# A fused two-block transformer kernel: block outputs on strips of 32 rows and seven pieces of work reordered in its second stage

## The reference

```python
q, gl, mq = split_cols(h @ w_in, [512, 24, 512])       # h: norm of x
k_c, v_c, k_s, v_s, k_w, v_w = rmsnorm(x, g_kv) @ w_kv
k_cmp, v_cmp = (gelu(blocks(a) @ w1) @ w2 for a in (k_c, v_c))   # 15 blocks, 2 groups
o = g0 * softmax(q k_cmp) v_cmp + g1 * softmax(q k_s) v_s + g2 * softmax(q k_w) v_w
m = softmax(mq mem_k) mem_v                            # 4 heads
x = x + concat([o, m]) @ w_out
```

## Time and profile before

| what | value |
|---|---|
| median of 3 runs | 894.53 us (894.26 to 894.65) |
| profiled execution, its own time | 893.82 us |
| span of its records | 892.1 us |
| TensorE busy | 885.8 us (99%) |
| VectorE busy | 648.7 us (73%) |
| ScalarE busy | 495.4 us (56%) |
| GpSimd busy | 44.3 us (5%) |

### The profile page before, as it was taken

One profiled execution on the slowest core, in us unless ns is written; L12 is line 12 of the kernel. 1 busy time (PEld: TensorE's weight loads), 2 busy tenths in 40 slices (PEclk: granted clock), 3 DMA queues, 4 the chain that ended last, 5 costly groups with the idle time before them and its releaser, 6 DMA issues.

```text
span 892.1 us, 18697 instructions
## 1 busy us (share of the span) xinstructions
PE 885.8 (99%) x7883; PEld 861.4 (97%) x7883; DVE 648.7 (73%) x1189; ACT 495.4 (56%) x851; POOL 44.3 (5%) x54
## 2 busy tenths in 40 slices
PE   8999999999999999999999999999999999999998
PEld 7999999999999998889999999999988999999998
DVE  6997657887767789785887767678688586565664
ACT  6763566564545566575565546547457464444451
POOL 1000001000000001000100000001142000000000
PEclk9999999999999999999999999999999999999999
DMA  8753343565465544632546554553162265546541
GB/s 324 287 189 113 126 174 134 211 243 190 155 227 187 187 151 160 242 124 97 213 181 243 205 200 176 213 211 129 64 235 96 96 228 201 195 181 217 199 152 48
DMA packets 26002, 160.68 MB, mean 180 GB/s; under 512 B 3008, under 2 KB 4928, under 8 KB 7360
## 3 DMA queue, kind: packets, MB, share of 16 engines
q1 hardware_dynamic: 25344, 158.45, 48.7%
q10 hardware_dynamic: 576, 1.05, 0.4%
HBM read 158.18 MB, written 1.05 MB: 178 GB/s over the span
## 4 chain that ended last, share of the span: by engine, by line
PE 94%; DVE 4%; ACT 1%; DMA 1%; issue 0%; SPq 0%
PE ps L417 92%; PE ps L433 2%; DVE wl L1291 1%; DMA xt<-in_x 1%; DVE xl L1299 1%; DVE arena L1741 0%; ACT coh L2097 0%; ACT wh L2085 0%; DVE xt L1487 0%; DVE col L1299 0%; ACT arena L2105 0%; DVE arena L1330 0%; DVE arena L1725 0%; DVE arena L1797 0%; DVE wl L1507 0%
## 5 line engine op out<-in xcount | busy, mean ns | idle before, releaser
L1291 DVE TENSOR_TENSOR wl<-raw,wh 128x1024 fp32r<-128x1024 f32 x280 | 329.5, 1224 | 120.8 <-ACT wh L2085 120.4
L417 PE MATMUL ps<-xh,wh 128*128 128x256 f32 (+1 forms) x1256 | 349.3, 278 | 0.6 <-DVE wl L1507 0.6
L417 PE MATMUL ps<-xl,wh 128*128 128x256 f32 (+1 forms) x1256 | 347.6, 277 | 0.0
L417 PE MATMUL ps<-xh,wl 128*128 128x256 f32 (+1 forms) x1256 | 347.6, 277 | 0.0
L2085 ACT CAST wh<-raw 128x1024 fp32r<-128x1024 f32 x280 | 277.3, 1048 | 115.3 <-PE ps L417 105.1
L417 PEld LDWEIGHTS ps<-xh,wh 128*128 128x128 f32 x1256 | 235.9, 188 | 2.0 <-DVE wl L1507 1.2
L417 PEld LDWEIGHTS ps<-xl,wh 128*128 128x128 f32 x1256 | 235.9, 188 | 0.0
L417 PEld LDWEIGHTS ps<-xh,wl 128*128 128x128 f32 x1256 | 235.9, 188 | 0.0
L417 PE MATMUL ps<-fh,wh 128*128 128x256 f32 x528 | 145.7, 276 | 0.0
L417 PE MATMUL ps<-fl,wh 128*128 128x256 f32 x528 | 145.7, 276 | 0.0
L417 PE MATMUL ps<-fh,wl 128*128 128x256 f32 x528 | 145.7, 276 | 0.0
(11 more groups left out here) (263 smaller groups left out, 1065.5 us busy)
## 6 DMA issues: line engine op xcount, KB each, us to landing
raw<-in_w SPq DMA_DIRECT2D x144, 1024.0 KB, 4.9
raw<-in_w ACTq DMA_DIRECT2D x4, 256.0 KB, 5.9
xt<-in_x SPq DMA_DIRECT2D x4, 256.0 KB, 6.6
raw<-in_w SPq DMA_DIRECT2D x4, 256.0 KB, 8.0
arena<-in_mem SPq DMA_DIRECT2D x1, 1024.0 KB, 8.4
out<-xt SPq DMA_DIRECT2D x8, 128.0 KB, 1.9
arena<-in_sel SPq DMA_DIRECT2D x3, 256.0 KB, 6.4
small<-in_small SPq DMA_DIRECT2D x1, 623.0 KB, 6.5
```

Of the source, the lines that this page charges most:

```text
L417: return pe.matmul(out, lhsT, rhs, start=start, stop=stop, skip_group_check=True)
L1291: v.tensor_tensor(L[:, s], src[:, s], f32(H[:, s]), ALU.subtract).then_inc(*w_lo.up(split(i, a)))
```

## The change

It makes these edits, all in layer B:

1. `blocks_out` issues eight products, each with 32 rows and 64 output columns, in place of four with 128 rows and 128 columns. `vcm` is one block of 64 columns, and the pairs stand in another order (`PLACE`, `slopes`, the gates), so that a strip of 32 rows holds one head of each half.
2. TensorE: both parts of `squeeze(1, ...)` stand ahead of scores 2; turn 2 stands between chunks 4, 5 and 6, 7 of Bm0; kvm follows in bank 6 with its value part first; output 2 stands ahead of `blocks_scores`. ScalarE's `squeezed(1)` moves ahead of the exponentials of pair 2.
3. TensorE's Bq0 reads chunks 0 and 1 from the original and in plain order; GpSimd's `first_two("B")` moves behind the zeroing of `pc_` and `vcm`.
4. VectorE's `rests("kvk", 2)` (the low part of kvv) moves behind the scaling of kvc and kvk.
5. The cast of Bo1 on ScalarE moves from behind `mem_exp(1, 1)` to behind `mem_turned(1, 1)`, and `mem_turned(1, 0)` to ahead of `mem_exp(1, 1)`. The low part of Bo1 on VectorE moves from behind `mem_probs(1, 1)` to between `mem_max(1, 3)` and `mem_probs(1, 2)`.

```diff
--- before.py
+++ after.py
@@ -297,7 +297,7 @@
     pc_ = cblk[:, 1024:1536]
     pc = v3(pc_, 32)[:, :, 0:15]
     kk, vv = area(512), area(512)
-    gT, kcm, vcm, gt, gh = area(120), area(16), area(256), area(48), area(512)
+    gT, kcm, vcm, gt, gh = area(120), area(16), area(256)[:, 0:64], area(48), area(512)
     PC2 = gh
     g4 = gT.rearrange("p (v c g n) -> p v c g n", v=2, c=2, g=2)
     gz = gh[:, 0:T]
@@ -898,6 +898,8 @@
                               False, False)
             last.then_inc(*n_pv.up(j))
 
+        PLACE = (0, 2, 1, 3)
+
         def blocks_scores(n, on):
 
             if n == 0:
@@ -909,7 +911,8 @@
             for j in range(4):
                 for g in range(2):
                     r = g * 64
-                    last = mm(ps[f"cs{g}"][:, n * 64 + j * 16:n * 64 + j * 16 + 15],
+                    at = n * 64 + PLACE[j] * 16
+                    last = mm(ps[f"cs{g}"][:, at:at + 15],
                               bq[r:r + 64, j, (1 - n) * 128:(2 - n) * 128], kcm[r:r + 64, 0:15], True, True)
                     if n == 1 and j == 3:
                         last.then_inc(*ps.full(f"cs{g}"))
@@ -926,12 +929,13 @@
         def blocks_out():
             t.wait_ge(*ps.done("kvm"))
             t.wait_ge(*ps.done("ct"))
-            for j in range(4):
-                name = f"no{j // 2}"
-                last = mm(ps[name][:, j % 2 * 256:j % 2 * 256 + 256], vcm[:, j % 2 * 128:(j % 2 + 1) * 128],
-                          PC2[:, j // 2 * 256:(j // 2 + 1) * 256], False, True)
-                if j % 2:
-                    last.then_inc(*ps.full(name))
+            for odd in range(2):
+                for n in range(4):
+                    name, r, g = f"no{n // 2}", n * 32, n % 2
+                    last = mm(ps[name][g * 64:(g + 1) * 64, odd * 256:(odd + 1) * 256], vcm[r:r + 32, :],
+                              PC2[r:r + 32, odd * 256:(odd + 1) * 256], False, True)
+                    if odd and g:
+                        last.then_inc(*ps.full(name))
 
         def out_b(c):
             return ps.done(f"mo1{c - 4}") if c >= 4 else ps.done(f"no{c // 2}")
@@ -941,7 +945,7 @@
         sums("B", 4)
         part_f("kvk", 1, range(4, 8), kv_in, CH, CL)
         norm_spread("B", 5, rst_)
-        unit_f("Bq0", 3, XH, XL, x_b, "B", (2, 3, 0, 1, 4, 5, 6, 7))
+        unit_f("Bq0", 3, XH, XL, x_b)
         P = ps.open("gates", 0)
         t.wait_ge(*ps.vacant("gates"))
         t.wait_ge(*s_wn.at(1))
@@ -965,8 +969,8 @@
         part_f("Bq1", 1, range(4, 8), x_b)
         nsa_out(1)
         squeeze(1, 0, 2)
+        squeeze(1, 1)
         nsa_scores(2)
-        squeeze(1, 1)
         part_f("Bm0", 1, range(0, 4), x_b, two="B")
         nsa_scores(3)
         P = ps.open("gT", 0)
@@ -977,22 +981,22 @@
         for n in range(4):
             last = mm(P[:, n * 30:(n + 1) * 30], gh[:, n * 128:(n + 1) * 128], blocks, True, True)
         last.then_inc(*ps.full("gT"))
-        part_f("Bm0", 1, range(4, 8), x_b)
-        P = ps.open("kvm", 2)
+        part_f("Bm0", 1, range(4, 6), x_b)
+        nsa_turn(2)
+        part_f("Bm0", 1, range(6, 8), x_b)
+        P = ps.open("kvm", 6)
         t.wait_ge(*ps.vacant("kvm"))
         t.wait_ge(*ps.done("gT"))
+        for n in range(4):
+            for c in range(2):
+                mm(P[n * 32:n * 32 + 15, 64:128], g4[:, 1, c, n % 2, :], sm("wcv2")[:, c * 64:(c + 1) * 64], c == 0, c == 1)
         for g in range(2):
             for c in range(2):
-                mm(P[g * 64:(g + 1) * 64, 0:15], sm("wck2")[:, c * 64:(c + 1) * 64], g4[:, 0, c, g, :], c == 0, c == 1)
-
-        for n in range(4):
-            for c in range(2):
-                last = mm(P[n * 32:n * 32 + 15, 64:128], g4[:, 1, c, n % 2, :], sm("wcv2")[:, c * 64:(c + 1) * 64], c == 0, c == 1)
+                last = mm(P[g * 64:(g + 1) * 64, 0:15], sm("wck2")[:, c * 64:(c + 1) * 64], g4[:, 0, c, g, :], c == 0, c == 1)
         last.then_inc(*ps.full("kvm"))
-        nsa_turn(2)
+        nsa_out(2)
         blocks_scores(0, (7, 0))
         blocks_scores(1, None)
-        nsa_out(2)
         mem_scores(1, 0, 4, mqB, qB)
         part_f("Bm1", 1, range(0, 4), x_b, two="B")
         nsa_turn(3)
@@ -1687,7 +1691,6 @@
         token_variance("B")
         for c in range(8):
             enter("B", c, xs[c], sm("gmix1", c, c + 1), XH(c), XL(c))
-        rests("kvk", 2)
         take("spread_B", rs_[:, 0:T], T)
         d.wait_ge(*ps.done("spread_B"))
         by_rs("kvc", kc, rs_[:, 0:T])
@@ -1695,6 +1698,7 @@
         v.tensor_copy(ev5, kc.rearrange("p (v m two) -> p v two m", two=2, m=128)).then_inc(*n_evn.up(0))
         by_rs("kvk", kk, rs_[:, 0:T])
         v.tensor_scalar(nrst, rst_[:, 0:2], -1.0, None, ALU.mult).then_inc(*n_ge.up(0))
+        rests("kvk", 2)
 
         def queries(n):
 
@@ -1772,8 +1776,8 @@
             v.reciprocal(sc8[:, 32:48], sc8[:, 16:32]).then_inc(*k_rec.up(0))
             d.wait_ge(*k_rec.at(0))
             for n in range(2):
-                w = sc8[:, 32 + n * 8:40 + n * 8].rearrange("p (j g) -> p j g", g=2)
-                gate = gt[:, n * 24:n * 24 + 24].rearrange("p (g j x) -> p j g x", g=2, j=4)[:, :, :, 0]
+                w = sc8[:, 32 + n * 8:40 + n * 8].rearrange("p (odd a g) -> p odd a g", a=2, g=2)
+                gate = gt[:, n * 24:n * 24 + 24].rearrange("p (g a odd x) -> p odd a g x", g=2, a=2, odd=2)[:, :, :, :, 0]
                 last = v.tensor_tensor(w, w, gate, ALU.mult)
             last.then_inc(*k_w.up(0))
             d.wait_ge(*k_w.at(0))
@@ -1830,8 +1834,8 @@
         v.tensor_copy(kcm[:, 0:15], ps["kvm"][:, 0:15])
         d.wait_ge(*n_zero.at(0))
         for n in range(4):
-            r, a = n * 32, n // 2 * 128 + n % 2 * 64
-            last = v.tensor_copy(vcm[r:r + 15, a:a + 64], ps["kvm"][r:r + 15, 64:128])
+            r = n * 32
+            last = v.tensor_copy(vcm[r:r + 15, :], ps["kvm"][r:r + 15, 64:128])
         last.then_inc(*ps.freed("kvm"))
         by_rs("Bm0", mqB_[:, 0:512], rs_[:, 0:T], 128.0 ** -0.5)
         nsa_probs(3)
@@ -1843,7 +1847,6 @@
         mem_max(1, 1, scB)
         by_rs("Bm1", mqB_[:, 512:1024], rs_[:, 0:T], 128.0 ** -0.5)
         mem_probs(1, 1, scB)
-        rests("Bm1", 2)
 
         def nsa_low(j):
             d.wait_ge(*n_hi.at(j))
@@ -1858,6 +1861,7 @@
         nsa_low(1)
         mem_max(1, 2, scB)
         mem_max(1, 3, scB)
+        rests("Bm1", 2)
         mem_probs(1, 2, scB)
         mem_low(1, 0)
         mem_probs(1, 3, scB)
@@ -2395,8 +2399,8 @@
         nsa_turned(1)
         casts("cv0", 2)
         squeezed(0)
+        squeezed(1)
         nsa_exps(2)
-        squeezed(1)
         gelu()
         casts("cv1", 2)
         nsa_exps(3, (0,))
@@ -2409,13 +2413,13 @@
         nsa_turned(3)
         a.wait_ge(*ps.ready("ct"))
         s.copy(PC2, ps["ct"][:, :]).then_inc(*ps.freed("ct"))
+        mem_turned(1, 0)
         mem_exp(1, 1, scB)
-        casts("Bm1", 2)
-        mem_turned(1, 0)
         nsa_high(0)
         nsa_high(1)
         mem_exp(1, 2, scB)
         mem_turned(1, 1)
+        casts("Bm1", 2)
         mem_high(1, 0)
         mem_exp(1, 3, scB)
         mem_high(1, 1)
@@ -2561,10 +2565,10 @@
         first_two("f0")
         token_power("f0")
         token_power("B")
-        first_two("B")
         q.wait_ge(*ps.ready("cmp0"))
         g.memset(pc_, 0.0)
         g.memset(vcm, 0.0).then_inc(*n_zero.up(0))
+        first_two("B")
         first_two("f1")
         token_power("f1")
         power("meta", rst_[0:NM, 2:3], rst_[0:NM, 10:11], ps.done("sums_meta"))
@@ -2697,7 +2701,7 @@
     cmp = [np.where(i * 128 + t - e >= 0, -(i * 128 + t - e), NEG) for i in (1, 0)]
     slope = lambda j, g: 2.0 ** -(g * 4 + j + 1)
     qs = np.array([[0.125 / slope(j, r // 64) for j in range(4)] for r in range(128)])
-    sl = np.broadcast_to(np.array([slope(j, g) for j in range(4) for g in range(2)]), (128, 8))
+    sl = np.broadcast_to(np.array([slope(j, g) for j in (0, 2, 1, 3) for g in range(2)]), (128, 8))
     ns = np.concatenate([-(128 + t - s), np.where(s <= t, -(t - s), NEG)] + cmp + [qs, sl], 1).astype(f)
     return cst, gm, ns, sel
```

## The result

The changed kernel takes 901.25 us (median of 4 executions, 898.88 to 903.85), the kernel before 894.39 us (894.24 to 894.65). The ratio is 1.0078, with a 95% interval of 1.0066 to 1.0090: slower, as forecast, but 6.9 us in place of 4.8, and just above the range.

The account below looks back on a forecast made before the run. The prediction took TensorE, busy 885.8 of 892.1 us, as the bound. Its terms 0.2 + 2.7 - 1.1 + 3.0 = 4.8 us, added to the 894.53 us median, gave 899.3 us, range 897.0 to 901.2.

Parts of the forecast that it names:

- A: Layer B's opening, edits 3 and 4: queries earlier, but GpSimd's copies slow VectorE's probabilities and split; turn 1 left 0.2 us later.
- B: Up to memory scores 0, edit 2: squeezes save 0.14 us, but kvm waits for ScalarE's copies of turn 2; 2.7 us later.
- C: Blocks' outputs, edit 1: eight products take 1.0 us instead of 2.00; with 0.1 before memory turn 0, 1.1 us less.
- D: Memory head 2, edit 5: Bo1's moved cast and split delay `mem_probs(1, 2)`; TensorE waits 3.0 us at memory turn 2.
- five steps: Chain after memory output 0, through Bo1's cast and split to `mem_probs(1, 2)`, each fixed by order, done 8.4 us later.
- Rival (3): Blocks' outputs: strips sharing a PSUM bank take turns, products need 2.0 us and win nothing; 900.3 us, 20%.
- (4): Behind the new waits TensorE's clock falls to 1.2 GHz, adding 3 us for a 3 us stretch; 902.3 us, 4%.

Follow-up runs that it names:

- Experiments 6: Edits 3 and 4 alone on the kernel before (GpSimd's copies behind the zeroing, VectorE's low part of kvv behind the scalings): 894.22 us against 894.27.
- 7: Edits 3 and 4 on the kernel before, with GpSimd's copies waiting until turn 1 is done: 893.86 us, ratio 0.9995.
- Experiment 12: The changed kernel with kvm in bank 7 in place of bank 6, nothing else: 899.07 us, ratio 1.0057 against the kernel before.
- experiments 2: The changed kernel with TensorE's order around kvm and the places of Bo1's cast and split put back: 897.02 us, ratio 1.0027 against the kernel before.
- 4: The changed kernel with TensorE's order around kvm alone put back: 899.81 us, ratio 1.0068 against the kernel before.
- 8: The kernel before with both parts of squeeze(1) ahead of scores 2, ScalarE's copy moved with them: 895.26 us, ratio 1.0019.
- Experiment 1: Edit 1 alone (blocks' outputs on strips of 32 rows) on the kernel before: 894.24 us against 894.28, ratio 1.0001.
- Experiment 3: The changed kernel with the cast and split of Bo1 alone put back: 898.35 us, ratio 1.0059 against the kernel before.
- Experiments 9: The kernel before with edit 1, earlier Bo1 cast and split, early copy of memory turn 0, and edits 3 and 4 with copies behind turn 1: 892.90 us.
- 10: The kernel before with edit 1, earlier Bo1 cast and split and early copy of memory turn 0, without edits 3 and 4: 893.12 us, ratio 0.9991.
- experiment 5: The changed kernel with unread products filling its waits, 19 before kvm and 26 before memory turn 2: 899.53 us, ratio 1.0069 against the kernel before.
- experiment 11: The kernel before with the block scores' products of 15 columns issued three times, no wait added: 900.83 us, ratio 1.0074.

## Why the prediction was right and where it failed

The steps, by the starts of the same work in the two profiled executions:

| step | forecast, us | trace, us |
|---|---|---|
| A, to the products behind turn 1 | +0.2 | +0.14 |
| B, to memory scores 0 | +2.7 | +4.13, of which 1.56 clock |
| C, to memory output 0 | -1.1 | -1.13 |
| D, to memory turn 2 | +3.0 | +3.03 |
| before layer B's spread | 0 | +0.61 |
| sum | +4.8 | +6.8 |

Without the clock's 1.56 and the start's 0.61, the steps sum to 4.6 us, against the 4.8 of the forecast.

**A** was right in both halves: 0.56 us won on the low parts, 0.54 lost on the probabilities beside the copies. The forecast looked for some of the loss in the split; that took 2.35 us as ever, only later, and TensorE waited 0.24 us for it. Experiments 6 and 7 show that the place of the copies decides the sign: +0.13 and -0.40 us in the traces.

**B** holds in its mechanism and size once the clock is taken out: 2.57 us against 2.7. Experiment 12 separates the bank from the copies. What the forecast passed over is a cost that was covered by this wait: joining the squeezes makes VectorE 0.9 us later, which experiments 2, 4 and 8 bring out. The sentence that a later scores 2 leaves ScalarE's chain where it is was true, but VectorE's was not asked about with kvm at its old place.

**C** held: eight products took 1.02 us. Rival (3), from the Trainium skill ("TensorEngine Tiling (Array Packing)", Restrictions and Gotchas), did not come about: strips 0 and 1, which write one bank in different columns of the array, start 7 ns apart. Experiment 1 adds that C needs both its parts; alone the strips gain nothing.

**D** held to 0.03 us, each of its five steps at its place. Experiment 3 shows that the move had a reason: at the old place, a wait of 1.1 us comes up behind the shortened blocks' outputs. Experiments 9 and 10 show the place that serves both.

**The step that failed is the assumption of a constant clock.** The sum of 4.8 has no term for it; a fall stands only among the rivals, as (4), with 4%. Its chance was read from a kernel in which TensorE had no such wait, and three of four executions fell. Two of these were at half clock for longer than the profiled one, by their mean clocks of 0.996 and 0.994 against 0.998. In the median the falls cost 901.25 less 898.88, 2.4 us. Rival (4) was mis-priced too: it adds 3 us for a stretch of 3 us. But a stretch at half clock does half of its length in work, so it costs the other half. The trace shows this: one stretch of about 3.4 us, of which 3.3 stand in the window above, and 1.56 us lost. In the one execution without a fall, the forecast is 0.4 us too high and the range holds the time.

What makes the clock fall is shown in part. Executions with a fall, by kernel:

| kernel | falls |
|---|---|
| before; experiments 1, 6, 7, 9, 10 | 0 of 64; 0 of 55 |
| experiment 8: 0.9 us wait before the block scores | 4 of 11 |
| experiment 2: the same, and a wait of 1.1 | 4 of 6 |
| changed kernel; experiments 3, 4, 12: a wait of 2.1 to 2.9 us | 3, 2, 4 and 2 of 4 |
| experiment 5: waits filled | 1 of 5 |
| experiment 11: no wait, 96 thin records | 4 of 4 |

A long wait goes with it: in experiments 4 and 12 the traces show the fall behind the second wait, among full-width products. Thin products go with it too: experiment 11 needs no wait at all, and a wait of 0.9 us goes with falls in front of thin products (8) and not in front of full ones (1). The block scores and part of kvm have 15 columns, and stand right behind the first wait. How much of each fall is due to either is not settled, and with four or five executions for most kernels the counts are rough.

## What to carry to other kernels

When work is moved to fill or save a few tenths on the bounding engine, follow each moved piece on the other engines' queues to the next thing that the bounding engine waits for: here 0.14 us saved cost 0.9, and 1.0 us saved needed one copy ahead of time. A piece that only has to be done some time belongs in the idle time that the timeline shows on its own engine, not between the links of a chain. And a wait of 2 to 3 us on TensorE is not priced by its length alone: look at the mean clock of each execution, not only at the median time. The same holds for a wait of 0.9 us in front of thin products (experiment 8).

## What was not expected of the hardware

- TensorE's clock fell to 1.2 GHz in a stretch in which the profile shows it busy all the time: 64 of 96 records of 15 columns had started, in 3.5 us, when the clock fell at 388.4; it stayed at half until 395.2 (experiment 11). With 32 such records and no wait near them no execution of the kernel before shows less than 0.999, and none was measurably longer for it.
- VectorE's products of two SBUF operands took 1.23 to 1.37 us a pair beside GpSimd's copies, and 1.03 alone; beside GpSimd's zeroing they were not slowed in the kernel before.
- Products on different strips of 32 rows and different halves of the columns write one PSUM bank side by side: 16 records of 256 columns in 1.02 us.
